# A fused two-block model on one core: attention scores from rounded high and low parts, with the copies of turned tiles and one subtraction placed anew

## The chip, the cores and the metric

The kernel runs on one core of one Trainium2 chip. The metric is the device time of one execution in microseconds (us). The kernel before took 2338.59 us, the median of three runs (2335.22 to 2341.79).

## What is computed

The model is two blocks after one another over 512 tokens of width 1024: an even layer, an odd layer, a mixing layer and a layer of experts. The change lies in the odd layer's attention. Its essence in the reference, for 12 heads of width 128 that share 2 heads of keys and values:

```python
qh = q.reshape(...).astype(jnp.float32) * (NSA_DH ** -0.5)
# per block of queries
ss = jnp.einsum('bghqd,bgqkd->bghqk', qb, kg) + bias_s      # selected keys
ps = masked_softmax(ss, (rel_s >= 0)[:, :, None])
osel = jnp.einsum('bghqk,bgqkd->bghqd', ps, vg)
sw = jnp.einsum('bghqd,bgkd->bghqk', qb, kwb) + head_bias(rel_w)   # window
pw = masked_softmax(sw, mask_w)
ow = jnp.einsum('bghqk,bgkd->bghqd', pw, vwb)
return gb[:, 0, ..., None] * oc + gb[:, 1, ..., None] * osel + gb[:, 2, ..., None] * ow
```

With 512 tokens the eight blocks of 64 keys that are selected are all there are, and the window of 512 reaches back to the first token. So both attentions are causal attention over all keys, with different keys and values (`ks`, `vs` and `kw`, `vw`). The third term `oc` is attention over 31 compressed keys. Computation is in fp32.

## The kernel before

The program is a row of stages that use the five engines in queues written out by hand: `mem_in, even_in, even_mix, even_out, odd_in, nsa, odd_out, mix_in, ssm, mix_mid, mix_out, moe`. Each stage builds on what the one before leaves in SBUF. The change is in `nsa` alone (L1890 to L2184). There is no planner in it: the order on each engine is that of its loop.

`nsa` begins with `MemAttention` (L1196), 16 small steps of another attention, into which `guest` functions weave the late projection of keys and the attention over compressed keys. Behind it comes the loop of the change. Its `steps` (L1916) are 12 heads by 4 tiles of 128 queries, 48 in all. I call the tiles t0 to t3. Tile t sees (t + 1) * 128 keys, so its scores are 128, 256, 384 or 512 columns wide. Two attentions run side by side in a step: index 0 is the selected one, index 1 the window.

A step passes through a pipeline that is spread over four turns `u` of the loop:

- PE (L2012 to L2055), in turn `u`: the scores of step u (L2024; fp32, one matmul per attention, in banks 2 * (u % 2) and the next), then the mix with the values of step u - 3 (L2039; t + 1 matmuls per attention into bank 6 or 7), then the transposes of the exponentials of step u - 2 (L2053; banks 4 and 5, t + 1 each).
- DVE (L2145 to L2182): the two row minima of step u, which at once add the bias and write the shifted scores to SBUF (L2155, a custom instruction and the reading of its accumulator), then the copy of the window's turned tile of step u - 2 out of bank 5 (L2164), then five small instructions that close step u - 3 (L2169 to L2182): the inverse of the sum, the gate, the two attentions added to `oc`, and the product with the output's gate.
- ACT (L2100 to L2108): the exponential of the selected attention of step u (L2089, with its row sum), the copy of the turned tile of step u - 2 out of bank 4 (L2097), the exponential of the window of step u.
- SP only fetches one row of biases per head (L1957).

What orders the work: scores of u wait until the minima of u - 2 are made (their banks), mixing waits for both copies (`cop_a` from ACT, `cop_v` from DVE) and for the closing of two steps earlier, transposes wait for the exponentials and for the copies that free banks 4 and 5, copies wait for the transposes (`turned`). The queries `k.qT` hold q with its sign turned, which is why minima take the place of maxima.

The program uses TensorE in two ways of reading fp32 data. An fp32 matmul is two instructions in the trace, each with a load of weights (the 96 score matmuls are 192 rows). The projections (L526, L528, L1572) split both operands beforehand into a rounded high part (a cast to `fp32r` on ACT, L488) and a low part (what is left, a subtraction on DVE, L493), and add three products: high by high, high by low, low by high. Each of these is one instruction.

The instruction of L1586 and L1601 is the same split elsewhere: a cast of 512 columns out of PSUM on ACT, and a subtraction of 512 columns on DVE.

## Time and profile before

| | |
|---|---|
| three runs, median (lowest to highest) | 2338.59 us (2335.22 to 2341.79) |
| the profiled execution: its own time | 2337.2 us |
| its span | 2334.7 us |
| PE busy | 2226.2 us (95%) |
| DVE busy | 821.2 us (35%) |
| ACT busy | 503.9 us (22%) |
| mean granted TensorE clock | 0.986 |
| the stage of the change | about 784 to 931 us |

The span is what the profiler saw of the program, first instruction to last; the execution's own time has 2.5 us more around it. PE's busy time counts modelled ends of pipelined matmuls, so a busy PE can still be waiting in small gaps; start times tell more than durations. On ACT and DVE an instruction may start before the one ahead of it has ended, so what an instruction costs its engine is the distance to the next start. The granted clock is a share of 2.4 GHz.

### The profile page before, as it was taken

Reading aid. Unit: us, or ns where it says so; the run is one execution under the profiler, and the core shown is the slowest. Engines: PE = TensorE matmul, PEld = TensorE weight load, DVE = VectorE, ACT = ScalarE, POOL = GpSimd, SP = SyncE. Lnnn points to the kernel's source line nnn. Section 1 sums busy time; section 2 is a strip of 40 time slices with the busy share of each in tenths; the row PEclk is TensorE's granted clock in tenths of the full one; section 3 lists DMA queues with packets and bytes.
Section 4 is the critical chain, followed back from the end, with each engine's and each line's share of the span. In section 5 each row is a group of like instructions: output and inputs, shape, how many; then the busy total and the mean of one; then the engine's idle time right before and its main releaser. Section 6 shows DMA issues by size and latency. Waiting matters only on the chain.

```text
span 2334.7 us, 32451 instructions
## 1 busy us (share of the span) xinstructions
PE 2226.2 (95%) x13844; PEld 1650.4 (71%) x13844; DVE 821.2 (35%) x1668; ACT 503.9 (22%) x885; POOL 209.7 (9%) x173
## 2 busy tenths in 40 slices
PE   8999999999999998999989999999999999998997
PEld 5889888888888777877877876555565555555553
DVE  6563245343225688453247561111111111111113
ACT  3222333231123554242224220000000000000001
POOL 0640000011100000660000000000000000000000
PEclk9999999999999999999999999999999999999999
DMA  8633222254331100445172789999999999999997
GB/s 260 224 129 126 72 85 91 100 167 145 113 107 28 41 24 13 174 140 167 59 165 91 260 345 408 426 427 427 427 426 426 428 426 426 427 426 427 426 427 314
DMA packets 123828, 573.29 MB, mean 246 GB/s; under 512 B 30487, under 2 KB 44427, under 8 KB 97783
## 3 DMA queue, kind: packets, MB, share of 16 engines
q1 hardware_dynamic: 110468, 533.21, 58.4%
q0 software_dynamic: 12064, 33.79, 4.1%
q10 hardware_dynamic: 1152, 4.19, 0.5%
q8 instruction: 112, 1.84, 0.3%
q14 instruction: 32, 0.26, 0.0%
HBM read 543.63 MB, written 39.47 MB: 250 GB/s over the span
## 4 chain that ended last, share of the span: by engine, by line
PE 28%; DMA 18%; DVE 3%; issue 1%; SPq 0%; ACT 0%; DVEq 0%
PE ps L3261 12%; DMA mem<-in_expert_w_down 9%; DMA mem_u<-in_expert_w_down 7%; PE ps L3288 7%; PE ps L3239 2%; PE ps L2896 2%; PE ps L2627 1%; PE ps L2594 0%; PE ps L2614 0%; DVE mem L2450 0%; PE ps L2945 0%; DVE mem L2472 0%; PE ps L2920 0%; DMA mem_u<-prep_w 0%; PE ps L3669 0%
## 5 line engine op out<-in xcount | busy, mean ns | idle before, releaser
L528 PE MATMUL ps<-w_parts,u_parts 128*128 128x512 f32 (+2 forms) x1920 | 414.7, 376 | 2.9 <-DVE u_parts L716 2.6
L528 PEld LDWEIGHTS ps<-w_parts,u_parts 128*128 128x128 f32 x1920 | 349.4, 188 | 61.3 <-DVE u_parts L716 3.1
L3261 PE MATMUL ps<-mem,mem_u 128*64 128x256 f32 x2464 | 291.4, 390 | 4.5 <-issue 2.9
L493 DVE TENSOR_TENSOR w_parts<-w_raw,w_parts 128x2048 fp32r<-128x2048 f32 (+2 forms) x70 | 163.7, 2338 | 320.4 <-ACT w_parts L488 320.3
L3384 DVE TENSOR_TENSOR mem_c<-mem_c,ps 128x256 f32<-128x256 f32 x64 | 27.0, 422 | 685.1 <-PE ps L3261 679.9
L3261 PEld LDWEIGHTS ps<-mem,mem_u 128*64 128x64 f32 x2464 | 181.7, 135 | 109.8 <-issue 17.2
L488 ACT CAST w_parts<-w_raw 128x2048 fp32r<-128x2048 f32 (+2 forms) x70 | 128.6, 1837 | 398.8 <-PE ps L528 166.3
L3288 PE MATMUL ps<-mem,mem_c 128*64 128x512 f32 x624 | 194.4, 623 | 20.1 <-DMA mem<-in_expert_w_down 12.7
L1572 PE MATMUL ps<-w_parts,u_parts 128*128 128x512 f32 x768 | 181.6, 393 | 0.4 <-DVE u_parts L1601 0.4
L1572 PEld LDWEIGHTS ps<-w_parts,u_parts 128*128 128x128 f32 x768 | 142.2, 188 | 29.8 <-issue 0.8
L526 PE MATMUL ps<-u_parts,w_parts 128*128 128x512 f32 x672 | 154.5, 390 | 1.7 <-DVE w_parts L493 1.7
L3288 PE MATMUL ps<-mem_u,mem_c 128*64 128x512 f32 x304 | 142.2, 623 | 6.7 <-DMA mem<-in_expert_w_down 5.1
L526 PEld LDWEIGHTS ps<-u_parts,w_parts 128*128 128x128 f32 x672 | 125.7, 188 | 29.4 <-DVE w_parts L493 2.1
L3261 PE MATMUL ps<-mem_u 128*64 128x256 f32 x1216 | 144.8, 388 | 1.0 <-DMA mem_u<-in_expert_w_up 1.0
L3336 ACT COPY mem_u<-ps 128x512 f32<-128x512 f32 x64 | 37.5, 585 | 478.1 <-PE ps L3288 478.1
L3288 PEld LDWEIGHTS ps<-mem,mem_c 128*64 128x64 f32 x624 | 60.5, 143 | 102.2 <-issue 97.3
L3239 PEld LDWEIGHTS ps<-picks,hn_parts 128*128 128x128 f32 x960 | 117.4, 191 | 16.6 <-issue 12.1
L3239 PE MATMUL ps<-picks,hn_parts 128*128 128x256 f32 x960 | 126.8, 287 | 1.6 <-DVE mem_u L3366 0.2
L3261 PEld LDWEIGHTS ps<-mem_u 128*64 128x64 f32 x1216 | 89.2, 134 | 51.5 <-issue 5.0
L3220 POOL DMA_INDIRECT y<-mem_u,mem_c x31 | 30.2, 975 | 892.0 <-ACT mem_u L3336 779.4
L3342 ACT ACTIVATE mem_c<-ps 128x256 f32<-128x256 f32 x64 | 24.5, 384 | 384.0 <-PE ps L3261 384.0
L2039 PEld LDWEIGHTS ps<-mem_u 128*128 128x128 f32 x480 | 59.0, 191 | 23.6 <-ACT mem_u L2097 15.2
(447 smaller groups left out, 2671.0 us busy)
## 6 DMA issues: line engine op xcount, KB each, us to landing
mem<-in_expert_w_gate SPq DMA_DIRECT2D x39, 2048.0 KB, 35.6
mem<-in_expert_w_up SPq DMA_DIRECT2D x38, 2048.0 KB, 39.8
mem<-in_expert_w_down SPq DMA_DIRECT2D x37, 2048.0 KB, 39.8
mem_u<-in_expert_w_up SPq DMA_DIRECT2D x26, 2048.0 KB, 39.6
mem_u<-in_expert_w_down SPq DMA_DIRECT2D x19, 2048.0 KB, 42.0
mem_c<-in_expert_w_gate SPq DMA_DIRECT2D x13, 2048.0 KB, 35.4
mem_u<-in_expert_w_gate SPq DMA_DIRECT2D x12, 2048.0 KB
w_raw<-in_od_w_in SPq DMA_DIRECT2D x21, 1024.0 KB, 5.1
```

The lines of the kernel that those rows point to most:

```text
L488: act.copy(self.part(n, 0), self.raw(n)).then_inc(self.high, 1)
L493: dve.tensor_tensor(self.part(n, 1), self.raw(n), self.part(n, 0).bitcast(F32), ALU.subtract).then_inc(self.low, 1)
L526: mm = pe.matmul(out, w[x][:, kk, g.t * P:(g.t + 1) * P], u[:, y, ku, :], start=first, stop=last)
L528: mm = pe.matmul(out, u[:, x, ku, g.t * P:(g.t + 1) * P], w[y][:, kk, :], start=first, stop=last)
L1572: mm = pe.matmul(k.ps[:, g.bank, :], parts[g.part // 2][:, x, ky, g.t * P:(g.t + 1) * P], w[z][:, kk, :], start=g.part == 0 and kk == 0 an ...
L2039: mm = pe.matmul(o[:, 128 * i:128 * i + 128], pT[v % 2][:, 512 * i + kt * P:512 * i + kt * P + P], vv[:, kt, g * DH:(g + 1) * DH], start=k ...
L2896: mm = pe.matmul(k.ps[:, 4 * n + m, :], mT_low[:, m, kk, :] if x else mT_high[:, kk, m * P:(m + 1) * P], w[z][:, kk, :], start=kk == 0 and ...
L3220: pool.indirect_dma_start(k.y_dram, bass.IndirectOffsetOnAxis(ap=k.slot_row[:, e:e + 1].bitcast(U32), axis=0), yn[:, e % STORES, :], None, ...
L3239: mm = pe.matmul(o, k.hn_parts[:, part, m, 2 * r + j, :], k.picks[:, m, :, :], start=m + part == 0, stop=m == NT - 1 and part == 1)
L3261: mm = pe.matmul(ps[SLOTS * h:SLOTS * (h + 1), bank, 0:256].rearrange("s (c j) -> s c j", j=2), x[:, kk, :], w[:, kk, :].rearrange("p (c h ...
L3288: mm = pe.matmul(ps[SLOTS * i:SLOTS * (i + 1), ROWS + c, :], aT[:, i, j, SLOTS * h:SLOTS * (h + 1)], w[i][:, h, j, 512 * c:512 * (c + 1)], ...
L3336: act.copy(yn[:, pair % STORES, 512 * c:512 * (c + 1)], ps[:, ROWS + c, :]).then_inc(rows_ready, 1)
```

## The change

Three things are altered, all in `nsa`.

1. For heads 1 to 11 and tiles t1 to t3 the scores are made from rounded parts: three `fp32r` products per attention instead of one fp32 matmul. Head 0 and tile t0 of each head stay as they were. The parts of the keys (2 attentions by 2 key heads, 512 columns each) are made once: ACT rounds them after the exponentials of turn 0 (`split_keys`), DVE subtracts in turn 1. The parts of q are made per head, in two buffers: ACT rounds the q of head h + 2 after the exponentials of tile t3 of head h (`split_head`; that of head 1 in turn 1), DVE makes the low part of head h + 1 behind the minima of tile t0 of head h (of t2 in head 0). They lie where the compressed attention's tables and some of the projection's outputs lay.
2. For tiles t0 and t1 ACT copies the turned tiles of both attentions in one instruction, ahead of its first exponential, and DVE copies nothing. For t2 and t3 both copy as before.
3. The counts that PE waits for follow from that (`by_dve`).

```diff
--- before.py
+++ after.py
@@ -1921,12 +1921,20 @@
     scored, low, exped, turned, cop_a, cop_v, mixed, stored = (
         k.sem("nsa_" + x) for x in ("scored", "low", "exped", "turned", "copied_act", "copied_dve", "mixed", "stored"))
     bias_loaded = [k.sem(f"nsa_bias{i}") for i in range(2)]
+    q_high, q_low, k_high, k_low = (k.sem("nsa_" + x) for x in ("q_high", "q_low", "keys_high", "keys_low"))
+    q_parts = [rounded(k, f"nsa_q_{x}", N0 + 1024 * i, 2, S) for i, x in enumerate(("high", "low"))]
+    k_parts = [rounded(k, f"nsa_keys_{x}", o, 2 * NKV, S) for x, o in (("high", Z0 + 11264), ("low", Z0 + 8192))]
+    PRODUCTS = ((0, 0), (0, 1), (1, 0))
 
     c_uses = [("score", t) for t in range(NT)]
     for at in ("turn", 0), ("turn", 1), ("mix", 0), ("turn", 2), ("mix", 1), ("turn", 3), ("mix", 2), ("mix", 3):
         c_uses += [at] if at[0] == "turn" else [("mix", at[1], q) for q in range(N_QUADS)]
     c_at = {("score", 0): 0, ("score", 1): 1, ("score", 2): 5, ("score", 3): 6, ("turn", 0): 8, ("turn", 1): 9,
             ("mix", 0): 11, ("turn", 2): 12, ("mix", 1): 13, ("turn", 3): 14, ("mix", 2): 16, ("mix", 3): 18}
+
+    def by_dve(v):
+        whole, rest = divmod(v + 1, NT)
+        return 2 * whole + max(0, rest - 2)
 
     def c_bank(use):
         return 6 + c_uses.index(use) % 2
@@ -2021,14 +2029,23 @@
                     if u >= 2:
                         pe.wait_ge(low, 2 * (u - 1))
                     for i, kT in enumerate((k.ksT, k.kwT)):
-                        pe.matmul(k.ps[:, 2 * (u % 2) + i, 0:m], k.qT[:, h, t * P:(t + 1) * P], kT[:, g, 0:m],
-                                  start=True, stop=True).then_inc(scored, 1)
+                        o = k.ps[:, 2 * (u % 2) + i, 0:m]
+                        if h == 0 or t == 0:
+                            mm = pe.matmul(o, k.qT[:, h, t * P:(t + 1) * P], kT[:, g, 0:m], start=True, stop=True)
+                        else:
+                            pe.wait_ge(k_low, 2 * NKV)
+                            pe.wait_ge(q_low, h)
+                            for x, z in PRODUCTS:
+                                mm = pe.matmul(o, q_parts[x][:, h % 2, t * P:(t + 1) * P],
+                                               k_parts[z][:, NKV * i + g, 0:m], start=x + z == 0, stop=x == 1)
+                        mm.then_inc(scored, 1)
                 if u >= 3:
                     v = u - 3
                     h, t = steps[v]
                     g = h // HPG
                     pe.wait_ge(cop_a, v + 1)
-                    pe.wait_ge(cop_v, v + 1)
+                    if by_dve(v):
+                        pe.wait_ge(cop_v, by_dve(v))
                     if v == 0:
                         pe.wait_ge(c_copied, c_number(c_uses[-1]))
                     if v >= 2:
@@ -2047,8 +2064,10 @@
                         pe.wait_ge(ma.stored, len(ma.steps))
                     for i in range(2):
                         pe.wait_ge(exped, 2 * v + 1 + i)
-                        if v:
-                            pe.wait_ge(cop_v if i else cop_a, v)
+                        if i and v and steps[v - 1][1] >= 2:
+                            pe.wait_ge(cop_v, by_dve(v - 1))
+                        elif v:
+                            pe.wait_ge(cop_a, v)
                         for kt in range(t + 1):
                             tr = pe.transpose(k.ps[:, 4 + i, kt * P:(kt + 1) * P],
                                               sc[v % 3][:, i, kt * P:(kt + 1) * P], k.ident)
@@ -2091,19 +2110,44 @@
 
             def take_turned(v):
                 w = (steps[v][1] + 1) * P
-                act.wait_ge(turned, 2 * v + 1)
+                both = steps[v][1] < 2
+                act.wait_ge(turned, 2 * v + 1 + both)
                 if v >= 2:
                     act.wait_ge(mixed, v - 1)
-                act.copy(pT[v % 2][:, 0:w], k.ps[:, 4, 0:w]).then_inc(cop_a, 1)
+                if both:
+                    act.copy(pT[v % 2].rearrange("p (i w) -> p i w", i=2)[:, :, 0:w], k.ps[:, 4:6, 0:w]).then_inc(cop_a, 1)
+                else:
+                    act.copy(pT[v % 2][:, 0:w], k.ps[:, 4, 0:w]).then_inc(cop_a, 1)
+
+            def split_keys():
+                act.wait_ge(ma.mixed, len(ma.steps))
+                for i, kT in enumerate((k.ksT, k.kwT)):
+                    for g in range(NKV):
+                        act.copy(k_parts[0][:, NKV * i + g, :], kT[:, g, :]).then_inc(k_high, 1)
+
+            def split_head(h):
+                if h >= 3:
+                    act.wait_ge(scored, 2 * NT * (h - 1))
+                act.copy(q_parts[0][:, h % 2, :], k.qT[:, h, :]).then_inc(q_high, 1)
 
             ma.scalar(act, guest)
             for u in range(n + 2):
+                turned_first = u >= 2 and steps[u - 2][1] < 2
+                if turned_first:
+                    take_turned(u - 2)
                 if u < n:
                     exponential(u, 0)
-                if u >= 2:
+                if u >= 2 and not turned_first:
                     take_turned(u - 2)
                 if u < n:
                     exponential(u, 1)
+                    h, t = steps[u]
+                    if u == 0:
+                        split_keys()
+                    if u == 1:
+                        split_head(1)
+                    if t == NT - 1 and h + 2 < NH:
+                        split_head(h + 2)
                 if u == n - 2 * NT:
                     k.out_pr.scalar_split(act, 0)
 
@@ -2155,11 +2199,20 @@
                         dve.tensor_tensor_reduce(sc[u % 3][:, b, 0:w], k.ps[:, 2 * (u % 2) + b, 0:w],
                                                  backwards(bias_n[:, h % 2, 0:w]), 1.0, 3e38, ALU.add, ALU.min,
                                                  st[:, u % 4, 0, b:b + 1]).then_inc(low, 1)
-                if 2 <= u < n + 2:
+                    if u == 1:
+                        for i, kT in enumerate((k.ksT, k.kwT)):
+                            for g in range(NKV):
+                                dve.wait_ge(k_high, NKV * i + g + 1)
+                                dve.tensor_tensor(k_parts[1][:, NKV * i + g, :], kT[:, g, :],
+                                                  k_parts[0][:, NKV * i + g, :].bitcast(F32), ALU.subtract).then_inc(k_low, 1)
+                    if t == (0 if h else 2) and h + 1 < NH:
+                        dve.wait_ge(q_high, h + 1)
+                        dve.tensor_tensor(q_parts[1][:, (h + 1) % 2, :], k.qT[:, h + 1, :],
+                                          q_parts[0][:, (h + 1) % 2, :].bitcast(F32), ALU.subtract).then_inc(q_low, 1)
+                if 2 <= u < n + 2 and steps[u - 2][1] >= 2:
                     v = u - 2
                     w = (steps[v][1] + 1) * P
-                    if v >= 2:
-                        dve.wait_ge(mixed, v - 1)
+                    dve.wait_ge(mixed, v - 1)
                     dve.wait_ge(turned, 2 * v + 2)
                     dve.tensor_copy(pT[v % 2][:, 512:512 + w], k.ps[:, 5, 0:w]).then_inc(cop_v, 1)
                 if u >= 3:
```

## Rows read from the trace of the kernel before

**Rows 1.** Stretches: length, busy PE, PEld, DVE, ACT, POOL; granted clock, DMA share, GB/s

```profile
784.00:931.00 147.00, 137.22 (x914) 112.27 (x912) 123.72 (x483) 75.09 (x242) 0.00 (x0) 1.00 0.09 26
1028.00:1036.00 8.00, 5.97 (x27) 4.79 (x26) 7.75 (x10) 7.38 (x13) 0.43 (x1) 0.79 0.23 66
```

**Rows 2.** Waits between 796 and 918 us: who waited, total, times, longest

```profile
DVE mem_u L2164 <- PE ps L2053: 12.3, 30, 0.6
```

**Rows 3.** One head in order of time: start, length, engine, line, operation, [idle before]

```profile
845.79 1.88 PE L2024 MATMUL ps<-mem_u 128*128 128x512 f32 x4
...
846.06 0.29 DVE L2164 COPY mem_u<-ps 128x128 f32<-128x128 f32 x1 [0.28 <-PE ps L2053]
...
847.51 0.61 PE L2039 MATMUL ps<-mem_u 128*128 128x128 f32 x4
...
847.96 0.60 PE L2053 MATMUL ps<-mem_c,mem_u 128*128 128x128 f32 x4
...
848.36 0.72 ACT L2089 ACTIVATE mem<-mem,mem_c 128x512 f32<-128x512 f32 x1 [1.56 <-DVE mem_c L2155]
848.39 0.61 PE L2024 MATMUL ps<-mem_u 128*128 128x128 f32 x4
...
849.08 0.35 ACT L2097 COPY mem_u<-ps 128x256 f32<-128x256 f32 x1
...
849.49 1.16 PE L2039 MATMUL ps<-mem_u 128*128 128x128 f32 x8 [0.48 <-ACT mem_u L2097]
...
851.41 0.56 DVE L2164 COPY mem_u<-ps 128x384 f32<-128x384 f32 x1 [0.34 <-PE ps L2053]
...
852.07 1.58 PE L2039 MATMUL ps<-mem_u 128*128 128x128 f32 x12
...
853.48 1.04 PE L2053 MATMUL ps<-mem_c,mem 128*128 128x128 f32 x8
...
854.35 1.46 PE L2024 MATMUL ps<-mem_u 128*128 128x384 f32 x4
854.62 0.69 DVE L2164 COPY mem_u<-ps 128x512 f32<-128x512 f32 x1 [0.60 <-PE ps L2053]
...
855.23 0.16 DVE L2169 RECIPROCAL mem_c<-mem_c 128x2 f32<-128x2 f32 x1
...
856.60 0.55 DVE L2155 CUSTOM_DVE_ANT_0 mem<-ps,mem_u 128x384 f32<-128x384 f32 x1
...
857.65 0.59 PE L2024 MATMUL ps<-mem_u 128*128 128x512 f32 x1
```

**Rows 4.** Rounded matmuls by form, 140 to 260 us: busy us, mean ns; last whole page

```profile
L528 PE MATMUL ps<-w_parts,u_parts 128*128 128x512 f32 x273 | 62.5, 389 | 0.0
L528 PE MATMUL ps<-w_parts,u_parts 128*128 128x384 f32 x192 | 33.7, 335 | 0.0
...
L3239 PE MATMUL ps<-picks,hn_parts 128*128 128x256 f32 x960 | 126.8, 287 | 1.6 <-DVE mem_u L3366 0.2
```

**Rows 5.** DVE and ACT by form; first ns min/median/max, then busy us, mean ns

```profile
L493 DVE TENSOR_TENSOR w_parts<-w_raw,w_parts x70: 1374/2292/4531, 66.3 to 1163.7; 128x2048 fp32r<-128x2048 f32 x60, 128x1536 fp32r<-128x1536 f32 x8, 128x1168 fp32r<-128x1168 f32 x2
...
L1601 DVE TENSOR_TENSOR u_parts<-ps,u_parts 128x512 fp32r<-128x512 f32 x32 | 21.4, 688 | 44.1 <-ACT u_parts L1586 44.1
...
L1586 ACT CAST u_parts<-ps 128x512 fp32r<-128x512 f32 x32 | 18.2, 590 | 60.7 <-PE ps L1557 60.7
...
L2097 ACT COPY mem_u<-ps 128x512 f32<-128x512 f32 x12 | 6.8, 566 | 2.6 <-PE ps L2053 2.6
```

**Rows 6.** The first steps of the stage, in order of time

```profile
785.80 0.49 ACT L2089 ACTIVATE mem_u<-mem_u,mem_c 128x256 f32<-128x256 f32 x1
...
786.20 0.56 DVE L2155 CUSTOM_DVE_ANT_0 mem<-ps,mem_u 128x384 f32<-128x384 f32 x1 [0.23 <-PE ps L2024]
...
792.12 0.56 DVE L2164 COPY mem_u<-ps 128x384 f32<-128x384 f32 x1 [0.25 <-PE ps L2053]
```

**Rows 7.** PE in order of time, around 1030 us

```profile
1030.62 4.51 PE L528 MATMUL ps<-w_parts,u_parts 128*128 128x512 f32 x12 [2.03 <-DVE u_parts L716]
```

## The prediction

> **What bounds the kernel now.** I first read the share of the engines over the stage of the change, 784 to 931 us [rows 1]. PE is busy for 137 of 147 us and DVE for 124, at the full granted clock and with almost no DMA. So it is two engines in step, and small waits decide. The waits inside it [rows 2] show DVE waiting 12.3 us for the transposes (L2053). Then I read one head, instruction by instruction [rows 3]: four steps, tiles t0 to t3 (t0 is 128 columns wide, t3 512). Scores of t3 start at 845.79 and again at 857.65, so a head takes 11.86 us. PE stands still in one place only: the four score matmuls of t0 start at 848.39 and fill some 0.45, but the mix of t1 starts at 849.49, as ACT's copy at 849.08 stood behind a 0.72 us exponential. That is 0.65 us, plus 0.06 ahead of 852.07; PE's own work is 11.86 - 0.71 = 11.15. DVE's waits are 0.28, 0.34 and 0.60 ahead of its three copies, with an accumulator read of 0.08 beside each: its work is 11.86 - 1.22 - 0.24 = 10.40.
>
> The head closes in two parts, both between DVE copies [rows 3]. From the copy of t3 (854.62) to that of the next t2 (851.41 + 11.86) it is 8.65 us, and PE's chain sets it. From the copy of t2 to that of t3 it is 3.21 us: copy, mix (L2039), transposes (L2053), strictly one after the other; scores lie beside it.
>
> **Scores on PE.** A 512 tile in fp32 takes 1.72 us for both keys (845.79 to 847.51), 384 and 256 in proportion 1.29 and 0.86 [rows 3]. A rounded matmul takes 62.5/273 = 0.229 us at 512 and 33.7/192 = 0.176 at 384; by the same step 0.123 at 256, and not over 126.8/960 = 0.132 [rows 4]. Six of them (three products, two keys) give 1.37, 1.06 and 0.74: saved 0.35, 0.23 and 0.12, in sum 0.70 us a head, in 11 heads. Head 0 and every t0 stay fp32. The Trainium skill, "FP8 and Floating Point Precision", section "TensorE Precision Notes", says that true FP32 takes four passes through the array. By that the three products would take three quarters of the time, 0.97 us less a head instead of 0.70; the rows have 0.229 where a quarter of the 0.86 us tile is 0.215. The sum would be 1.2 us lower at most, through ACT's chain below.
>
> **Copies.** For t0 and t1 ACT now copies both banks, ahead of its exponential, and waits for both to be turned. Behind that wait stand the exponentials of t2 and t3, started up to 0.8 us later than now; their transposes come some 3 us after their minima, so nobody waits. The transposes of t1 end at 847.96 + 0.60, 0.17 after 848.39; ACT starts 0.10 later (as DVE does from 853.48 + 1.04 to 854.62), copies 512 columns in 0.57 [rows 5], and PE follows 0.06 later: the mix of t1 begins 0.89 to 0.90 after the scores instead of 1.10, 0.21 saved [rows 3]. A copy from two banks at once is not in the trace: its bounds are 0.35 (256 columns, 849.08) and twice that, and I take the 0.57 of a copy of as many columns from one bank.
>
> **DVE.** A copy of 512 columns is 0.69 long and holds DVE 0.61 (854.62 to 855.23), 0.08 less; 128 columns take 0.29 and 384 take 0.56, so 256 take 0.42 [rows 3]. It loses two copies a head, 0.21 and 0.34, and gains one subtraction of 512 columns, 0.688 long [rows 5], which holds it 0.61. Work goes from 10.40 to 10.46: nothing is gained there. But the place changes: from the copy of t3 to that of t2 it works 8.65 - 0.62 - 0.16 = 7.87, then 7.87 - 0.55 + 0.61 = **7.93**. PE's chain over the same part is 8.65 - 0.23 - 0.35 - 0.21, plus 0.07 because the shorter scores of t2 no longer quite cover the 0.69 copy of t3: also **7.93**. A tie; the scores of t1 (0.12) lie off both.
>
> **ACT.** The rounding of the next q is a cast of 512 columns, 0.590 from PSUM [rows 5], holding ACT about 0.50 (849.08 + 0.35 overlaps its follower by 0.09 or so, an estimate). It stands after t3's exponentials. From the turned t1: copy 0.47, exponentials 0.72 + 0.72, cast 0.50, first exponential of t0 0.40 (0.72 less 384 columns at the (0.57 - 0.35)/256 of its copies), in sum 2.81; then its copy of t2, 0.46 between those two, and 0.06 let PE go at 3.33. DVE's copy lets it go at 0.62 (mix of t1 begins) + 1.00 (eight matmuls of 0.11, and 0.11 for late weights) + 0.82 (six transposes by 853.48's eight) + 0.10 + 0.56 + 0.10 = 3.20. ACT is 0.13 later where it casts (before copies of t2 in heads 1 to 9).
>
> **Period:** 7.93 + 3.21 + 0.13 = 11.27, or 11.14 in the last two heads. Gain: 9 x 0.59 + 2 x 0.72 = **6.7 us**. The new waits of PE (keys and q low) ask for parts made a head earlier and cost nothing. No DMA, no SP or POOL queue is touched; the cast of an output weight on ACT and its subtraction on DVE near the end stand behind the same steps as before.
>
> **Start, once.** ACT rounds both keys' four parts where it now begins the exponential of t1, at 785.80; DVE subtracts behind it, 4 x 0.61, until 788.9, where it began the minima of t2 at 786.20 [rows 6]. Then two minima of t2 0.95 (each holds DVE as a copy of its width), low part of q 0.61, minima of t3 1.22, the closing five instructions of t0 1.37 (855.23 to 856.60), minima of t0 0.42, low part 0.61 and 0.1 of waiting for ACT: copy of t2 at 794.2 instead of 792.12. **+2.1 us**; the waits that DVE had there, 0.23 and 0.25 among them [rows 6], are spent in it.
>
> **Sum:** -6.7 + 2.1 = -4.6 us. All later stages start from the end of this one, so it is carried through. The profiled execution took 2337.2 us (span 2334.7), 1.4 under the median of 2338.6 of the three runs; it would take 2332.6, the median 2334.0, 0.2% less. About 0.3%, 7 us, is what a measurement here can tell from no change.
>
> **Rivals.**
> - *The waits go too.* Then a head is the work of PE (11.15 - 0.70 = 10.45) or DVE (10.46): 11 x 1.40 - 2.1 = 13.3 us, 2325.3. For: the two engines would be matched. Against: copy, mix, transposes and copy of t3 follow one another whatever the scores cost. 0.17, with what lies between.
> - *ACT becomes the bound.* It gets a cast and wider copies, and t2's copy is not ahead of the exponential. If two banks take 0.70 and the cast waits or runs longer, 0.4 more a head, the gain is 0.2 a head: no net change, 2338.6. For: it is already last by 0.13. Against: it is busy for half of the stage [rows 1]. 0.13.
> - *Slower: the subtractions.* Both operands and the result lie in SBUF, and that form has a maximum of 4531 ns beside a median of 2292 [rows 5]. At twice the time each holds DVE 0.60 longer, ahead of the copy of t2: 11 x (0.60 - 0.13) = 5.2 us of the gain, and 6 x 0.60 = 3.6 at the start: 2338.6 - 4.6 + 8.8 = 2342.8. It turns the sign once a low part takes about 0.35 longer, from 0.96 us on. For: the stage rests on DVE's order. Against: half of that line's 70 instances stand at 2292 or under, and few transfers run in this stage, 26 GB/s [rows 1]. 0.07.
> - *The clock.* After 2.03 us of idle PE [rows 7] the granted clock is 0.79 over 8 us, part of it at 1.2 GHz [rows 1], and 12 matmuls take 4.51 us instead of 12 x 0.229 = 2.75. In the start PE will wait some 1.2 us for the first copy. Against: 0.65 us of idle in every head leaves the clock at 1.00 over the whole stage [rows 1], and 1.2 is nearer to that. If it fell: +1.8, 2335.8. The Trainium skill, "TensorE: Matmul & The Clock Gate", section "What's actually happening", has the clock follow how busy PE was; the trace agrees. 0.05.
> - *The order does nothing.* If the copy of t1 is not earlier, DVE's tied chain still sets 7.93 + 0.21 at worst: 2336.3. Within the forecast's width.
>
> **Numbers.** Forecast 0.58, the rest as above. The predicted time is the forecast's. Range 2328.5 to 2341: it takes in half of the first rival, ACT, the clock and a low part up to about 0.5 us longer; a period wrong by 0.4 either way is 4.4 us. Faster by over 0.3% (below 2331.6): nearly all of the first rival and an eighth of the forecast, 0.25. Slower by over 0.3%: only the far end of the subtractions and what I don't see, 0.04. Within: 0.71.
>
> **What would show it.** Right: rounded score matmuls of 0.23, 0.18 and 0.12; a head of 11.2 to 11.3; PE's wait before the mix of t1 down from 0.65 to about 0.45 and a new one of 0.4 to 0.5 before that of t2, ended by ACT's copy; DVE waiting only ahead of the copy of t3, about 0.8; copy of t2 of head 0 near 794.2; end of the stage near 926.6. Wrong: a head under 11.0 or over 11.5, a low part over 0.75 us, a granted clock under 1.00 in the stage, or a later stage that does not keep the shift.

## The result, and the profile after

The changed kernel took 2342.70 us, the median of 21 runs (2337.95 to 2346.34). The kernel before took 2338.59 us, again the median of 21 (2334.42 to 2343.57). The ratio is 1.0017, with a 95% interval of 1.0010 to 1.0024. The forecast was 2334.0 in a range of 2328.5 to 2341.0: the time moved the other way, by 4 us, and lies outside the range.

The profiled execution of the changed kernel took 2346.34 us. First the page, its span and busy times:

```profile
span 2344.2 us, 32632 instructions
...
PE 2225.8 (95%) x13910; PEld 1660.5 (71%) x13910; DVE 821.9 (35%) x1659; ACT 515.0 (22%) x900; POOL 210.2 (9%) x173
```

The share of the engines over the stage, to be held against [rows 1] (columns as there):

```profile
787.00:933.00 146.00, 131.93 (x982) 120.24 (x981) 124.27 (x471) 85.90 (x257) 0.00 (x0) 1.00 0.09 27
```

PE lost 5.3 us of busy time, where the forecast took 11 x 0.70 = 7.7 off its work, and ACT gained 10.8. DVE is where it was. The stage itself hardly became shorter. Its ends are the first minima and the last of the 48 closings (the product that ends a step). First the two rows of the kernel before, then those of the changed one, with its first copy of t2:

```profile
784.69 0.28 DVE L2155 CUSTOM_DVE_ANT_0 mem_u<-ps,mem_u 128x128 f32<-128x128 f32 x1
```

```profile
L2182 DVE TENSOR_TENSOR mem<-mem,mem_u x48: 291/292/293, 791.2 to 930.9; 128x128 f32<-128x128 f32 x48
```

```profile
L2235 DVE TENSOR_TENSOR mem<-mem,mem_u x48: 291/292/294, 796.0 to 933.9; 128x128 f32<-128x128 f32 x48
```

```profile
787.93 0.28 DVE L2199 CUSTOM_DVE_ANT_0 mem_u<-ps,mem_u 128x128 f32<-128x128 f32 x1
...
797.36 0.55 DVE L2217 COPY mem_u<-ps 128x384 f32<-128x384 f32 x1
```

From the first minima to the start of the last closing it is 933.9 - 787.9 = 146.0 us. Before, those two starts are 784.7 and 930.9, 146.2 apart. So attention gained 0.3 us of the 4.6 that were forecast. Behind the stage, from the start of the last closing to the end of the span, the kernel before had 2334.7 - 930.9 = 1403.8 us and the changed one has 2344.2 - 933.9 = 1410.3: 6.5 us more, where nothing was changed. Ahead of the stage the profiled execution is 3.2 us longer. That is not the change's: in `r1_cast_low_kk_late` below, which has the same instructions up to there, the stage begins at 783.6, and in `p2_after_pad59` at 787.2. Single executions differ there. So the two profiled executions are 9.5 us apart, where the medians are 4.1 apart, and only the parts can be compared. Two things are to be explained, then: a stage that gained nothing, and some 6 us lost behind it.

**One head.** The rows of the changed kernel that answer to [rows 3], in order of time:

```profile
847.77 0.69 DVE L2217 COPY mem_u<-ps 128x512 f32<-128x512 f32 x1 [0.60 <-PE ps L2072]
...
850.56 0.48 PE L2039 MATMUL ps<-nsa_keys_high,nsa_q_high 128*128 128x512 f32 x1
...
852.03 0.60 PE L2056 MATMUL ps<-mem_u 128*128 128x128 f32 x4
...
852.91 0.61 PE L2034 MATMUL ps<-mem_u 128*128 128x128 f32 x4
853.11 0.59 ACT L2118 COPY mem_u<-ps 128x512 f32<-128x512 f32 x1 [0.69 <-PE ps L2072]
...
853.75 1.16 PE L2056 MATMUL ps<-mem_u 128*128 128x128 f32 x8 [0.23 <-ACT mem_u L2118]
...
854.87 0.29 DVE L2199 CUSTOM_DVE_ANT_0 mem_u<-ps,mem_u 128x128 f32<-128x128 f32 x1
855.01 0.60 ACT L2131 CAST nsa_q_high<-mem_u 128x512 fp32r<-128x512 f32 x1
...
855.65 0.69 DVE L2210 TENSOR_TENSOR nsa_q_low<-mem_u,nsa_q_high 128x512 fp32r<-128x512 f32 x1 [0.48 <-ACT nsa_q_high L2131]
...
855.92 0.46 ACT L2120 COPY mem_u<-ps 128x384 f32<-128x384 f32 x1
...
856.26 0.55 DVE L2217 COPY mem_u<-ps 128x384 f32<-128x384 f32 x1
...
856.91 1.58 PE L2056 MATMUL ps<-mem_u 128*128 128x128 f32 x12 [0.64 <-ACT mem_u L2120]
...
859.47 0.69 DVE L2217 COPY mem_u<-ps 128x512 f32<-128x512 f32 x1 [0.60 <-PE ps L2072]
```

A head now takes 859.47 - 847.77 = 11.70 us, against 11.86. Between the copy of t2 and that of t3 it is 3.21, as forecast. Between the copy of t3 and that of t2 it is 8.49, where 7.93 + 0.13 = 8.06 was forecast. And in that part stands a wait that the forecast does not have: DVE makes the low part of the next q directly behind the minima of t0, and ACT rounds that same q directly ahead of it. PE then waits 0.64 us for the mix of t2. Its row names ACT's copy, but that had ended at 855.92 + 0.46 = 856.38; DVE's copy ended at 856.81, 0.10 ahead of PE's start, so it is DVE that PE waits for. DVE's wait over the whole stage, in total, times and longest:

```profile
DVE nsa_q_low L2210 <- ACT nsa_q_high L2131: 4.4, 9, 0.5
```

**Behind the stage.** The chain of waits of the state-space stage, kernel after (start, length, what), at its 128 short fp32 matmuls, L2433, which are 256 matmul rows in the trace:

```profile
1195.10 9.48 PE ps L2433 x228
1204.58 5.75 issue
1210.33 1.76 PE ps L2433 x28
1212.09 2.94 PE ps L2443 x7
```

The same matmuls of the kernel before, PE in order of time:

```profile
1191.39 7.33 PE L2380 MATMUL ps<-mem_c,mem_u 128*64 128x64 f32 x198 [2.25 <-DMA mem_u<-prep_w]
1199.82 1.91 PE L2380 MATMUL ps<-mem_c,mem_u 128*64 128x64 f32 x58 [1.11 <-issue]
1203.13 7.17 PE L2390 MATMUL ps<-mem,mem_u 128*128 128x256 f32 x32 [1.40 <-DVEq L2468]
```

In the middle of a row of independent matmuls PE stands still for 5.75 us and waits for nothing that the profile shows. Before, there was such a pause too, of 1.11 us, and it cost nothing, since the next matmuls (L2390) waited 1.40 for DVE anyhow. From the first short matmul to the next kind it is 1203.13 - 1191.39 = 11.7 us before and 1212.09 - 1195.10 = 17.0 after, 5.3 us of the 6.5. The windows of the changed kernel around it (columns as in [rows 1]) show what PE's neighbours did:

```profile
1200.00:1205.00 5.00, 4.58 (x142) 4.44 (x138) 3.15 (x3) 0.00 (x0) 0.00 (x0) 0.91 1.16 210
1205.00:1210.00 5.00, 0.00 (x0) 0.00 (x0) 4.75 (x5) 0.00 (x0) 0.00 (x0) 0.77 1.26 95
1210.00:1215.00 5.00, 4.67 (x36) 4.05 (x37) 4.93 (x3) 0.59 (x1) 0.00 (x0) 0.55 1.28 98
```

The clock follows the idle stretch down: it is granted at 0.55 over the five microseconds behind it, mostly the lower level of 1.2 GHz. And the DMA engines are full but move only 95 GB/s: these are the eight loads of the lags (`mem<-prep_kk`), in 4096 pieces of 512 bytes. Instructions arrive beside them, as the page's list of DMA queues says:

```profile
q8 instruction: 113, 1.85, 0.3%
```

113 packets of 16 KB; before it were 112. The change adds 197 rows to PE's record (66 loads of weights, 66 matmuls, 65 waits), so that each later instruction stands further back in this stream. Counted over PE's record in order of time, the pause comes at row 12993 before and at row 13249 after. These differ by exactly 256, so it is likely the same place in a packet; but it is row 397 of the 512 that the short matmuls make before, and row 456 after. The beginnings of the packets fit this. Counted from 0, packet n begins when PE is at row 256n + 150 to 200, in 38 of the first 49 packets of either kernel. By that, packet 49 of the kernel before was due at 1194.0, when PE was 100 rows into the short matmuls, and it began at 1197.25. Packet 50 of the changed kernel was due 160 rows in, at 1199.3, and began at 1207.01.

### The profile page after: what moved, and what is told of

The parts are those of the page before. It is cut to its first block, busy times and chain, and to the rows that moved or that the text cites. A ratio compares the mean times of both kernels' runs of the same rounds, so it can differ in the third digit from the quotient of the medians.

```text
span 2344.2 us, 32632 instructions
## 1 busy us (share of the span) xinstructions
PE 2225.8 (95%) x13910; PEld 1660.5 (71%) x13910; DVE 821.9 (35%) x1659; ACT 515.0 (22%) x900; POOL 210.2 (9%) x173
## 4 chain that ended last, share of the span: by engine, by line
PE 30%; DMA 18%; DVE 1%; issue 1%; ACT 0%; DVEq 0%; SPq 0%
PE ps L3314 12%; DMA mem<-in_expert_w_down 9%; PE ps L3341 7%; DMA mem_u<-in_expert_w_down 7%; PE ps L3292 2%; PE ps L2949 2%; PE ps L2680 1%; PE ps L2452 1%; PE ps L2469 1%; PE ps L2433 0%; PE ps L2647 0%; PE ps L2667 0%; PE ps L2998 0%; PE ps L2973 0%; PE ps L2443 0%
## 5 line engine op out<-in xcount | busy, mean ns | idle before, releaser
L3341 PE MATMUL ps<-mem_u,mem_c 128*64 128x512 f32 x304 | 140.1, 615 | 9.0 <-DMA mem<-in_expert_w_down 7.4
L3292 PEld LDWEIGHTS ps<-picks,hn_parts 128*128 128x128 f32 x960 | 117.5, 191 | 16.6 <-issue 12.2
L2056 PE MATMUL ps<-mem_u 128*128 128x128 f32 x480 | 64.5, 281 | 14.1 <-ACT mem_u L2120 9.6
```

Of the source, the lines that this page charges most:

```text
L2056: mm = pe.matmul(o[:, 128 * i:128 * i + 128], pT[v % 2][:, 512 * i + kt * P:512 * i + kt * P + P], vv[:, kt, g * DH:(g + 1) * DH], start=k ...
L3292: mm = pe.matmul(o, k.hn_parts[:, part, m, 2 * r + j, :], k.picks[:, m, :, :], start=m + part == 0, stop=m == NT - 1 and part == 1)
L3341: mm = pe.matmul(ps[SLOTS * i:SLOTS * (i + 1), ROWS + c, :], aT[:, i, j, SLOTS * h:SLOTS * (h + 1)], w[i][:, h, j, 512 * c:512 * (c + 1)], ...
```

## The experiments

Theories at the outset: (A) the stage gains little since DVE waits for ACT's cast; (B) behind it, PE starves for a block of instructions whose place the change has moved. Rivals: ACT itself is the bound of the head; the subtraction disturbs; behind the stage, the time at which the work comes, or the clock, and not the place in the stream.

### First four: the low part and the cast moved, and instructions that were none

`p1_before_pad197` and `p2_after_pad59` add no-operations to PE's queue at the program's start (197 to the kernel before, 59 to the changed one):

```diff
+            for _i in range(59):
+                pe.nop(nofuse=True)
             pe.wait_ge(ident_loaded, 16)
```

> The kernel before with 197 instructions that do nothing on PE, placed at its very start, where PE waits from 0.7 to 7.3 us for its first data. 197 is what the change adds to PE's stream. Theory of the packets (PE's instructions come in packets of 16 KB, 256 at a time, and where a packet ends inside the 512 quick instructions of the ssm stage sets how long PE starves there): PE's longest gap inside those matmuls goes from 1.1 us to 5 to 6 us, and the time rises by 3 to 5 us (ratio 1.0013 to 1.002), though the attention stage stays at 146.3 us. Rival, chance and clock: the gap is as often short as long in either kernel; no gap beyond 2 us here that belongs to the padding, ratio within 0.0007 of 1. Rival, the change's own stage costs the time: ratio 1.

> The changed kernel with 59 empty PE instructions at the start, so that 197 + 59 = 256 and packets end again where they ended in the kernel before. Theory of the packets: PE's gap in the ssm stage is back at about 1.1 us, and only the attention stage's own 0.3 us of gain is left: ratio 0.9995 to 1.0003 to the kernel before. Rival, the stage or anything behind it is slower by itself: the ratio stays at 1.0013 to 1.002.

Measured: p1 2338.18 us, ratio 1.0002 [0.9994, 1.0011], no pause over 0.1 us in the short matmuls, head 11.86, 1405.6 us behind the stage. p2 2341.75 us, ratio 1.0011 [1.0001, 1.0022], pause 5.7 us at row 13249 as without them, 2343.4 - 933.1 = 1410.3 us behind the stage. Both expectations missed, since the no-operations moved nothing: the packets are 112 and 113, and the pause of p2 stands at the very row. So neither run tests the place. They are repeats of the two kernels, and as such say that the pause comes with the change (and that the kernel before can be without any).

`p3_low_later` moves only the low part of the next q, from behind the minima of t0 to behind those of t1. `p4_cast_low_later` also moves ACT's rounding, from behind the exponentials of t3 to behind those of the head's own t0. Both also have the 59 no-operations, which do nothing.

```diff
-                    if t == (0 if h else 2) and h + 1 < NH:
+                    if t == (1 if h else 2) and h + 1 < NH:
```

```diff
-                    if t == NT - 1 and h + 2 < NH:
-                        split_head(h + 2)
+                    if t == 0 and h and h + 1 < NH:
+                        split_head(h + 1)
```

> The changed kernel with those 59, and with the subtraction for the next head's q behind the minima of tile t1 in place of t0 (head 0 as it was). Theory: in the changed kernel DVE waited 0.57 us in each head for ACT's cast, which is issued just ahead of it, in front of the copy of t2. A tile later the cast is long done and DVE fills the wait ahead of the copy of t3. A head goes from 11.70 to 11.25 to 11.30 us, the stage from 146.0 to about 141.5, ratio 0.9975 to 0.9985. Rival, the wait is on PE's chain anyway: a head stays at 11.6 to 11.7, ratio as with 59 alone.

> As the run before, and ACT casts the next head's q after the exponentials of its own head's tile t0 (for the next head) in place of after t3's (for the head after the next), where ACT otherwise waits for minima. Theory: ACT's copy of t2 is then no longer 0.13 us behind DVE's; a head takes 11.10 to 11.20 us, the stage about 140.5, ratio 0.997 to 0.998. Rival, ACT is not on the path: same as the run before within 0.03 us a head.

DVE's copies and low parts in p3, in order of time:

```profile
852.69 0.56 DVE L2219 COPY mem_u<-ps 128x384 f32<-128x384 f32 x1 [0.50 <-PE ps L2074]
855.22 0.69 DVE L2212 TENSOR_TENSOR nsa_q_low<-mem_u,nsa_q_high 128x512 fp32r<-128x512 f32 x1
...
863.95 0.56 DVE L2219 COPY mem_u<-ps 128x384 f32<-128x384 f32 x1 [0.51 <-PE ps L2074]
```

and in p4:

```profile
852.43 0.56 DVE L2219 COPY mem_u<-ps 128x384 f32<-128x384 f32 x1 [0.50 <-PE ps L2074]
...
863.54 0.56 DVE L2219 COPY mem_u<-ps 128x384 f32<-128x384 f32 x1 [0.50 <-PE ps L2074]
```

DVE's wait for the cast is gone in both, a head takes 863.95 - 852.69 = 11.26 us in p3 and 863.54 - 852.43 = 11.11 in p4, and the stage 141.4 and 140.1 us. Theory A holds: 0.44 us of each head was DVE's wait, and another 0.15 the cast ahead of ACT's copy of t2. The subtraction lasts 0.69 us wherever it stands. The heads came as expected, the ratios (0.9975 to 0.9985 and 0.997 to 0.998) did not. The times: p3 2338.62 us, ratio 1.0003 [0.9994, 1.0013]; p4 2337.15 us, ratio 0.9996 [0.9985, 1.0006]. The stage of p4 is 6.1 us shorter than before and the total is not, since behind the stage both have the pause (5.4 and 5.5 us).

### Second four: the place in the stream, and the transfers beside it

`q1_after_60ahead` and `q2_before_196ahead` add real instructions: transposes of a 32-row piece of the identity, two PE instructions each, where PE waits for its first input. `q3_cast_low_60ahead` is p4's order with 30 of them.

```diff
             pe.wait_ge(ident_loaded, 16)
+            for _i in range(30):
+                pe.transpose(k.ps[:, 7, 256:288], k.ident[0:32, :], k.ident[0:32, 0:32])
```

(98 in q2.) `q4_after_kk_late` moves no PE instruction. It holds back the loads of the lags until the short matmuls are done:

```diff
             kk = k.kk_dram.rearrange("c (g s) -> c g s", g=SG)
+            sp.wait_ge(s_ok, 2)
             for j in range(L):
```

> The changed kernel with 30 idle transposes of the identity (60 PE instructions) at the program's start, where PE waits for its first input anyway, so that each later PE instruction stands at the place in the instruction stream that it has in the kernel before, to within a few. Theory A, position: PE fetches its instructions in blocks of 256, the request for the block that is crossed late in the 128 short matmuls of the state-space stage comes 1.2 us earlier, ahead of the slow small transfers that begin there, and the pause in them falls from 5.8 us to 1.3 at most; time 0.997 to 0.9995 of the changed kernel's own, so ratio to before 0.997 to 1.000. Theory B: the pause comes from the shift in time of all later work against the transfers, not from position; it stays at 5 to 6 us, ratio 1.001 to 1.002. Attention stage unchanged, 145.9 to 146.0 us, under both.

> The kernel before with 98 idle transposes (196 PE instructions) at the program's start, so that each PE instruction from the end of attention on stands where it stands in the changed kernel. Theory A, position: a pause of 5 to 6 us appears in the short matmuls of the state-space stage, a further stretch at half clock behind it, and the ratio is 1.0015 to 1.0025, with attention unchanged at 146.2 us. Theory B, timing of the work: no pause over 1.3 us, ratio 0.999 to 1.001. Were the transposes themselves to cost something, it would show ahead of attention.

> The changed kernel with both the low part and its cast moved later (a head of 11.1 us was measured for that), and 60 PE instructions ahead. Theory A, position: pause of 1.3 us at most, so the 5.9 us gained in attention reach the end with 4.5 to 6 us more from the stage behind: ratio 0.9965 to 0.9985, under both kernels. Theory B: pause stays at 5 to 6 us, ratio 0.9990 to 1.0000 as without the instructions ahead.

> The changed kernel, with SP's eight loads of the kernel lags (small pieces, slow transfers) held until the 128 short matmuls are done. Contention: the instruction block was late because it stood behind these loads, so the pause in the matmuls falls to 1.5 us or less although no PE instruction has moved; the loads then land 10 us later and their readers wait, so the total is 2 to 10 us longer. Rival, the fetch is late by itself wherever the block boundary stands there: the pause stays at 5 to 6 us.

| | median us | ratio, 95% interval | pause us | behind the stage us |
|---|---|---|---|---|
| q1 | 2337.34 | 0.9995 [0.9984, 1.0006] | none | 1405.2 |
| q2 | 2348.62 | 1.0045 [1.0031, 1.0059] | 5.8 | 1410.2 |
| q3 | 2332.35 | 0.9977 [0.9966, 0.9988] | 2.3 | 1402.3 |
| q4 | 2338.59 (one run) | | none | 1403.3 |

PE in order of time, q1:

```profile
1189.86 10.34 PE L2435 MATMUL ps<-mem_c,mem_u 128*64 128x64 f32 x256 [2.24 <-DMA mem_u<-prep_w]
1202.86 8.60 PE L2445 MATMUL ps<-mem,mem_u 128*128 128x256 f32 x32 [2.65 <-DVEq L2523]
```

The chain of waits, q2 (the kernel before, with instructions ahead):

```profile
1202.58 9.20 PE ps L2382 x228
1211.78 5.75 issue
1217.54 1.76 PE ps L2382 x16
```

q4, PE in order of time, then the windows around it:

```profile
1194.54 9.95 PE L2434 MATMUL ps<-mem_c,mem_u 128*64 128x64 f32 x256 [3.33 <-DMA mem_u<-prep_w]
1207.24 6.96 PE L2444 MATMUL ps<-mem,mem_u 128*128 128x256 f32 x31 [2.75 <-DVEq L2522]
```

```profile
1200.00:1205.00 5.00, 4.49 (x155) 4.35 (x150) 4.03 (x4) 0.00 (x0) 0.00 (x0) 1.00 0.11 43
1205.00:1210.00 5.00, 2.76 (x13) 2.45 (x14) 4.78 (x4) 1.17 (x2) 0.00 (x0) 1.00 0.92 104
```

Theory B holds from both sides. Sixty more instructions ahead take the pause out of the changed kernel (with the shorter attention of q3, down to 2.3 us, and at the row within the short matmuls that it has in the kernel before); 196 put it into the kernel before, at the row of the changed one, with the same 5.75 us, and attention as it was. The time at which the work comes does not decide: p3 and p4 begin their short matmuls at 1190.6 and 1188.3 and have the pause, p1 and q1 begin at 1190.0 and 1189.9 and have none. Nor does a lower clock: p1 and q1 run these matmuls at the lower level for longer than the kernel before. And the pause is gone as well when nothing is moved but the loads of the lags (in q4, one run; r1 below has 0.6): so the long pause needs these loads beside the block. The position alone does nothing (q4), nor do the loads alone (q1); the two have to meet. The packets in the trace say by how little they do. In the kernel before the packet begins at 1197.25 and the pieces of 512 bytes at 1198.33. In the changed one these begin at 1201.33, and the packet only at 1207.01. In q1 it is 1195.79 and 1196.70, the packet ahead again. In q3 it is 1191.60 and 1191.69, only just ahead, and the pause is 2.3 us. A packet that begins ahead of the pieces costs 0 to 2.3 us in these runs; one caught behind them costs 3.2 (r3) to 5.75. The packet of the changed kernel was due 2.0 us ahead of them and was caught all the same.

Three expectations missed. The pause of q3 is 2.3 us and not 1.3 at most. q2 is slower than 1.0025: 98 transposes take longer than PE's initial wait. Ahead of attention it is 10 us later, and behind the stage 1410.2 us as the changed kernel, 6.4 more than before. So its ratio is not the price of the pause, which is read from the trace only. And q4 was expected 2 to 10 us longer, since the loads would land late. They did not matter: held back, they took 11.8 us each instead of 16.4 to land, the last at 1227.3, and their readers began at 1229.1, against 1235.1 in the changed kernel. Kernel after, then q4:

```profile
DMA to landing us min/median/max: 15.6/16.4/20.5
```

```profile
DMA to landing us min/median/max: 5.4/11.8/15.4
```

q3 shows that both causes add up: with attention at 140.1 us it is faster than both kernels.

### Third four: sum of both, and the parts of the change alone

`r1_cast_low_kk_late` is p4's order (without no-operations) with q4's edit, `r2_before_kk_late` the kernel before with q4's edit. `r3_scores_only` has the change's rounded scores but the old copies; `r4_copies_only` its copies but fp32 scores, and makes no parts. The core of each, r3 and then r4:

```diff
-                both = steps[v][1] < 2
+                both = False
-                turned_first = u >= 2 and steps[u - 2][1] < 2
+                turned_first = False
-                if 2 <= u < n + 2 and steps[u - 2][1] >= 2:
+                if 2 <= u < n + 2:
```

```diff
-                        if h == 0 or t == 0:
+                        if True:
```

> Low part behind the minima of t1, cast behind the head's own t0, and the loads of the kernel lags held until the short matmuls are done, with no instructions added ahead. If attention (6 us) and the late instruction block (5 to 6 us) are two separate causes, they add: pause of 1.5 us or less, attention stage 140.1 us, ratio 0.9965 to 0.9980. Rival, what held loads give is only the chance of one run: 0.999 to 1.000 as with the same attention order alone.

> The kernel before with the loads of the kernel lags held in the same way. Theory: the block was late by 1.1 us at most there, so little is to be had, ratio 0.9985 to 1.0005, and no pause over 0.3 us. Rival, holding these loads gains by itself (less traffic beside the matmuls) and would have given as much to the kernel before: 0.996 to 0.998.

> The change with its rounded scores but the old copies (ACT one bank, DVE the other, for every tile, ACT behind its first exponential). DVE then has the subtraction of 0.61 and its wait of about 0.57 for the cast on top of all its old copies: the part of a head from the copy of t3 to that of t2 is 7.9 + 0.6 + 0.6 = 9.1 instead of 8.65, a head 12.2 to 12.3 us, the stage 151 to 152.5 us; with the late instruction block the ratio is 1.004 to 1.006. Rival, PE sets the head (its scores 0.58 shorter in this part): 11.3 to 11.6 us.

> The change with its copies ahead of the exponential (both banks on ACT for t0 and t1) but all scores in fp32 and no parts. PE's chain loses what the mix of t1 waited: 0.2 to 0.26 a head, DVE has 0.55 a head less to do and hides all of that: a head 11.60 to 11.66 us, the stage 143.3 to 144 us, ratio 0.998 to 0.9995, and the pause in the short matmuls that of the kernel before, 1.1 us or none. Rival, the copies change nothing since the exponentials behind them now come late: 11.86, ratio 1.000.

| | median us | ratio, 95% interval | stage us | pause us | behind the stage us |
|---|---|---|---|---|---|
| r1 | 2333.36 | 0.9978 [0.9969, 0.9987] | 140.2 | 0.6 | 1404.3 |
| r2 | 2338.42 | 1.0006 [0.9994, 1.0018] | 146.2 | 1.0 | 1404.8 |
| r3 | 2345.76 | 1.0029 [1.0018, 1.0040] | 150.5 | 3.2 | 1408.6 |
| r4 | 2335.51 | 0.9989 [0.9979, 0.9999] | 143.9 | 1.9 | 1404.2 |

Over all fourteen profiled executions: the eight with a pause of 2.3 us or less have 1402.2 to 1405.6 us behind the stage, the five with one of 5.4 to 5.75 have 1409.1 to 1411.0, and r3 lies between.

r1 against the rival: the held loads are worth what they take out. Order alone (p4) gave 0.9996, with the loads held 0.9978. r2: the same edit gives the kernel before nothing, as expected, since it had hardly a pause on its chain. Its pause of 1.0 stayed all the same, against the expectation of 0.3 at most, so the loads are not the whole reason why a block can be late: there it had landed at 1197.99 and PE stopped at 1198.18 and went on at 1199.44, 1.45 behind the landing. r4 too has a longer pause, 1.9 us, than the 1.1 that was expected.

r4, DVE's copies in order of time:

```profile
840.83 0.69 DVE L2201 COPY mem_u<-ps 128x512 f32<-128x512 f32 x1 [0.60 <-PE ps L2072]
849.21 0.56 DVE L2201 COPY mem_u<-ps 128x384 f32<-128x384 f32 x1 [0.94 <-PE ps L2072]
852.43 0.69 DVE L2201 COPY mem_u<-ps 128x512 f32<-128x512 f32 x1 [0.60 <-PE ps L2072]
```

A head of 852.43 - 840.83 = 11.60 us: the copies alone are worth 0.26 a head, and beat the whole change. Here PE's chain sets the head and DVE waits 0.94 ahead of the copy of t2. r3, DVE:

```profile
837.35 0.69 DVE L2215 COPY mem_u<-ps 128x512 f32<-128x512 f32 x1 [0.60 <-PE ps L2069]
...
845.27 0.28 DVE L2196 CUSTOM_DVE_ANT_0 mem<-ps,mem_u 128x128 f32<-128x128 f32 x1
845.48 0.69 DVE L2207 TENSOR_TENSOR nsa_q_low<-mem_u,nsa_q_high 128x512 fp32r<-128x512 f32 x1
846.09 0.55 DVE L2215 COPY mem_u<-ps 128x384 f32<-128x384 f32 x1
...
849.29 0.69 DVE L2215 COPY mem_u<-ps 128x512 f32<-128x512 f32 x1 [0.61 <-PE ps L2069]
```

849.29 - 837.35 = 11.94 us here, 11.88 in most heads. The expected 12.2 to 12.3 was wrong: I had charged this order with the wait for the cast too, and it has none. ACT, without the wider copy ahead of its exponentials, reaches the cast at 844.55, 0.9 before DVE wants it. What is left is that DVE, now the bound from the copy of t3 to that of t2 (8.74 us, without a wait), eats all that PE saves. So the rounded scores alone are worth nothing (0.02 a head lost in most, 0.3 in two, and 3.4 us at the start, where head 0 closes 18.7 us behind the first minima instead of 15.3), the copies alone 0.26, and together in the order of p4 0.75: the copies take 0.55 of work from DVE, about what the subtraction of 0.61 needs.

## Why the prediction was wrong

**Right.** The rounded scores one by one: 0.23 us each at 512 columns, 0.18 at 384, 0.12 at 256. The first of each six takes some 0.1 longer, though (850.56 to 852.03 for six is 1.47, forecast 1.37; 1.14 against 1.06 for t2), so that PE's work fell by about 0.48 us a head and not by 0.70: 11 x 0.48 = 5.3, as the stage shows. That size was off, and cost the forecast nothing that shows, since p4's head of 11.11 is that of the sum. The part from the copy of t2 to that of t3, 3.21. The copy from both banks, 0.48 to the next start where 0.47 was taken. The earlier mix of t1: 853.75 - 852.91 = 0.84 behind the scores, forecast 0.89, and r4 has the gain by itself, 0.26. The start: the copy of t2 of head 0 comes 797.36 - 787.93 = 9.4 us behind the first minima, in the kernel before 792.12 - 784.69 = 7.4, so 2.0 later, forecast 2.1. The price of the subtraction (0.69, held 0.61) and the granted clock of 1.00 in the stage: the rivals of the subtraction and of the clock fall. ACT's lateness of 0.13 from the cast ahead of t2's copy: p3 to p4, 0.15. By the four passes that the Trainium skill ("FP8 and Floating Point Precision", "TensorE Precision Notes") gives for true FP32, one product would take a quarter of the 0.86 us tile, 0.215, an estimate; it measured 0.23.

**The first step that failed** is the period, in the term "7.87 - 0.55 + 0.61 = **7.93**" for DVE, with 0.13 for ACT. The sum charged DVE with the subtraction's time and ACT with the cast's, each on its own engine, and said that the new waits "ask for parts made a head earlier and cost nothing". That holds of PE's waits. It does not hold of DVE's wait for the cast: `split_head(h + 2)` at the end of head h is two heads ahead only by its index. The loop counts steps by scores, so it runs between the scores of t3 of head h and those of t0 of head h + 1, whose low part (for h + 2) DVE makes next. Cast and subtraction are neighbours, and the cast stands behind two exponentials of 0.72. The forecast placed the cast in ACT's chain (its 0.47, 0.72 and 0.72 ahead, then 0.50) and did not lay DVE's chain beside it. Measured: 0.48 idle in nine heads, 4.4 us; a head of 11.70 against 11.27. The wait of 0.4 to 0.5 that the forecast saw ahead of the mix of t2, ended by ACT's copy, was 0.64, and it was DVE's copy that ended it. Without this wait p3 has 11.26, p4 11.11, against the forecast's 11.27 with and 11.14 without ACT's lateness. So the sum was right but for the wait it left out. Of the 6.7 us of gain 2.3 were left: the eleven distances from copy of t3 to copy of t3 add up to 131.9 us before and 129.7 after. The later start took 2.0 of these.

**The second step that failed** is one sentence: "All later stages start from the end of this one, so it is carried through." PE's 66 added matmuls with their loads and waits moved the instruction stream by 197 rows, and 270 microseconds behind the stage a block that came due beside the loads of the lags was late. That cost 5.75 us of pause, 2.65 to 2.75 of which would have been waited for DVE anyway (q1 and q4 have that wait instead), and a longer stretch at half clock behind it: 0.77 and 0.55 are granted in the ten microseconds from 1205, where q1 has 0.74 and 0.92 in those from 1200. Behind the stage it is 6.5 us against the kernel before, 5.1 against q1. This sets the sign of the result: without the pause (q1) the ratio is 0.9995. No rival had it; the prediction names a later stage that does not keep the shift only as a sign of being wrong. In the trace of before there was one row that could have led there: 1.11 us of PE waiting for "issue" in the middle of independent matmuls.

**The rivals.** "ACT becomes the bound" came nearest: at 0.4 more a head it gave no net change, and this is what the stage shows. But its price came from elsewhere, from the order of cast and subtraction, not from a slow copy of two banks. The chance for slower by over 0.3%, 0.04, was for what I did not see; the result is slower by 0.17%, within that bound but outside the range. Both failed steps are omissions of waits.

## What to carry to other kernels

Where a change adds a producer on one engine and its consumer on another, lay both queues side by side at that place: two costs that each fit can still be in the wrong order, and moving the consumer by one step (p3), and the producer by one as well (p4), cost nothing here. Added instructions can cost time far behind the change. If a stage behind has PE waiting for "issue" in a dense row of short instructions beside loads in small pieces, look at it first, and compare kernels by stage before blaming the edit. The versions that combine the two lessons (r1, ratio 0.9978; q3, 0.9977) are faster than both kernels.

## What the runs showed of the hardware

PE's instructions arrive during the run, in packets of 16 KB, one for some 256 recorded instructions, in a DMA queue beside those of the data. 256 such rows of short matmuls (128 matmul rows with their loads) took 5.1 us in the kernel before, 6.3 in the changed one, and 3.8 where the granted clock was 1.00. Where the next packet met the eight loads in pieces of 512 bytes (DMA share 1.26 at 95 GB/s) it began 5.7 us after these had begun, and PE stood still for 5.75 us. PE began again 1.4 to 1.8 us after the packet had landed (1199.82 after 1197.25 + 1.03 before; 1210.33 after 1207.01 + 1.75). With these loads held back the packet began at 1200.57 in q4 and PE did not stop.

Why the kernel before pauses for about 1 us in some executions (1.1; 1.0 in r2) and not in others (p1) can be read from the granted clock. The windows from 2.6 to 5.6 us behind the first short matmul, kernel before and p1 (columns as in [rows 1]):

```profile
1194.00:1197.00 3.00, 3.00 (x104) 3.00 (x102) 0.24 (x1) 0.00 (x0) 0.00 (x0) 0.95 0.93 388
```

```profile
1192.60:1195.60 3.00, 3.00 (x62) 3.00 (x61) 0.00 (x0) 0.00 (x0) 0.00 (x0) 0.50 0.95 393
```

The packet landed 6.9 and 6.8 us behind the first short matmul, and PE went on at 8.4 in the kernel before. At the higher clock it had used up what it had at 7.1 and stood still. In p1, at half clock for longer, it came to that row only at 8.4, when the next instructions were there. q1 is as p1. What is not in the trace is when a packet is asked for, only when it begins.

No-operations in PE's queue moved neither the packets' count nor the place of the pause; thirty small transposes at the program's start, in PE's first wait, did, and nothing was lost ahead of attention (it began at 784.2, in the kernel before at 784.7). Ninety-eight cost 10 us there.
